# A ninth 2 MB weight slot in a fused two-block kernel, and the first gate half of the experts loaded early

## What is computed

```python
gate = jnp.minimum(xe @ w_gate[e] + b_gate[e], SWIGLU_LIMIT)
up = jnp.clip(xe @ w_up[e] + b_up[e], -SWIGLU_LIMIT, SWIGLU_LIMIT)
act = (up + 1) * (gate * jax.nn.sigmoid(SWIGLU_ALPHA * gate))
return act @ w_down[e] + b_down[e]
```

## Time and profile before

| | |
|---|---|
| median of 3 runs | 1897.9 us (1896.06 to 1900.59) |
| span of the profiled execution | 1896.8 us |
| TensorE busy | 1800.5 us (95%) |
| VectorE, ScalarE busy | 769.7 us (41%), 597.2 us (31%) |
| read from HBM | 560.58 MB |
| first products of the experts, last down products end | 323.5 us, 1250.5 us |

### The profile page before, as it was taken

The page is one execution under the profiler, slowest core; times in us unless marked ns, Lnnn a source line. Parts: engine busy times, 40 slices in busy tenths (PEclk is TensorE's granted clock), DMA queues, the critical chain, the costliest instruction groups (busy, mean ns, idle before and its releaser), DMA issues.

```text
span 1896.8 us, 24863 instructions
## 1 busy us (share of the span) xinstructions
PE 1800.5 (95%) x10374; PEld 1111.5 (59%) x10374; DVE 769.7 (41%) x1339; ACT 597.2 (31%) x1076; POOL 20.4 (1%) x59
## 2 busy tenths in 40 slices
PE   6999999999999999999999999989999999989999
PEld 4987786333333333333333333358799997779998
DVE  2654664231322321222212222154664555646454
ACT  4455564111110111101111011045554445555443
POOL 0020010000000000000000000000000000000000
PEclk9999999999999999999999999999999999999999
DMA  8745446999999999999999999975346464325550
GB/s 306 254 159 192 170 184 262 411 428 426 428 427 427 428 427 427 428 426 428 427 428 428 427 428 428 427 268 178 133 141 207 141 218 160 133 89 179 177 200 23
DMA packets 122050, 563.27 MB, mean 297 GB/s; under 512 B 7216, under 2 KB 53424, under 8 KB 97360
## 3 DMA queue, kind: packets, MB, share of 16 engines
q1 hardware_dynamic: 121104, 558.70, 73.7%
q10 hardware_dynamic: 832, 2.95, 0.4%
HBM read 560.58 MB, written 1.05 MB: 296 GB/s over the span
## 4 chain that ended last, share of the span: by engine, by line
PE 74%; DMA 20%; DVE 3%; ACT 2%; issue 1%; SPq 0%; ACTq 0%; DVEq 0%
PE ps L1082 16%; DMA ring<-in_w_up 13%; PE ps L653 12%; PE ps L654 12%; PE ps L655 12%; PE ps L1117 8%; DMA arena<-in_w_up 5%; PE ps L1023 2%; PE ps L1043 2%; DMA ring<-in_w_ada 1%; PE ps L665 1%; PE ps L971 1%; PE ps L1004 1%; PE ps L758 1%; DMA ring<-in_w_in 1%
## 5 line engine op out<-in xcount | busy, mean ns | idle before, releaser
L653 PE MATMUL ps<-part,part 128*128 128x256 f32 (+2 forms) x1592 | 513.0, 322 | 7.1 <-DVE part L1989 4.3
L654 PE MATMUL ps<-part,part 128*128 128x256 f32 (+2 forms) x1592 | 502.5, 316 | 0.0
L655 PE MATMUL ps<-part,part 128*128 128x256 f32 (+2 forms) x1592 | 502.2, 315 | 0.0
L1082 PE MATMUL ps<-ring,arena 128*64 128x512 f32 x1536 | 342.4, 599 | 30.5 <-DMA ring<-in_w_up 30.2
L1989 DVE TENSOR_TENSOR part<-ring,part 128x1024 fp32r<-128x1024 f32 (+2 forms) x299 | 313.3, 1089 | 122.1 <-ACT part L1449 121.3
L653 PEld LDWEIGHTS ps<-part,part 128*128 128x128 f32 (+1 forms) x1592 | 305.1, 192 | 40.9 <-issue 13.2
L655 PEld LDWEIGHTS ps<-part,part 128*128 128x128 f32 (+1 forms) x1592 | 304.6, 191 | 19.3
L654 PEld LDWEIGHTS ps<-part,part 128*128 128x128 f32 (+1 forms) x1592 | 305.3, 192 | 17.2
L1449 ACT ACTIVATE part<-ring 128x1024 fp32r<-128x1024 f32 (+2 forms) x299 | 271.8, 948 | 32.2 <-PE ps L655 18.9
L1082 PEld LDWEIGHTS ps<-ring,arena 128*64 128x64 f32 x1536 | 115.1, 138 | 255.1 <-issue 254.6
L1986 DVE TENSOR_SCALAR arena<-ps 64x512 f32<-64x512 f32 x128 | 88.2, 689 | 375.9 <-PE ps L1082 370.3
(11 more groups left out here) (250 smaller groups left out, 1190.7 us busy)
## 6 DMA issues: line engine op xcount, KB each, us to landing
ring<-in_w_gate SPq DMA_DIRECT2D x48, 2048.0 KB, 26.4
ring<-in_w_up SPq DMA_DIRECT2D x48, 2048.0 KB, 29.2
ring<-in_w_down SPq DMA_DIRECT2D x48, 2048.0 KB, 27.3
ring<-in_ffn_w_in SPq DMA_DIRECT2D x44, 1024.0 KB, 7.8
arena<-in_w_gate SPq DMA_DIRECT2D x16, 2048.0 KB, 26.3
arena<-in_w_up SPq DMA_DIRECT2D x16, 2048.0 KB, 29.7
arena<-in_w_down SPq DMA_DIRECT2D x16, 2048.0 KB, 27.1
ring<-in_w_ada SPq DMA_DIRECT2D x12, 2048.0 KB, 10.6
```

The lines of the kernel that those rows point to most:

```text
L653: e.matmul(out, x[0], y[0], start=first, stop=False, skip_group_check=True)
L654: e.matmul(out, x[0], y[1], start=False, stop=False, skip_group_check=True)
L655: return e.matmul(out, x[1], y[0], start=False, stop=last, skip_group_check=True)
L1082: i = e.matmul(PS[p + h][CAP * r:CAP * r + CAP, :], xg[:, k0 + k, :], W(("moe_" + "gu"[r], ex, k0))[:, k, 512 * h:512 * h + 512], start=False,
```

## The change

A ninth slot. `spare_slot`, a tile of its own, becomes slot 6, and the two in the arena become 7 and 8. Its 16 KB per partition come from three places: the block of 128 columns of ones in the table of constants (readers now take the single column `one`, with stride 0 where 128 are wanted), 160 columns at the end of the tile `small`, and the scratch of the dynamic DMAs, cut to 1024 bytes. The cycle of the experts is `(6, 4, 0, 3, 5, 2, 1, 7, 8)`, starting behind 6 and 4. The first gate half goes to slot 6, which no one has used, and its load is put in the hand-written list between the `vb` slab and `ada` 6; slot 4, where it was, takes the first up half.

```diff
-for _name, _n in (("ident", 128), ("ones", 128), ("cos2", 128), ...
+for _name, _n in (("ident", 128), ("cos2", 128), ...
...
-        small = sb("small", [128, 640])
+        small = sb("small", [128, 480])
         ringt = sb("ring", [128, NSLOT, SLOT])
+        spare_slot = sb("spare", [128, SLOT])
...
-        more = []
+        more = [spare_slot]
...
-                    ("in", "qb"), ("ada", 5, 1), ("in", "ga0"), ("in", "vb"), ("ada", 6, 0), ("in", "ga1"), ("ada", 7, 1),
+                    ("in", "qb"), ("ada", 5, 1), ("in", "ga0"), ("in", "vb"), ("first", 0, 6), ("ada", 6, 0), ("in", "ga1"), ("ada", 7, 1),
...
-                    ("out", 0, 2), ("o", "ob", 0), ("first", 0, 4), ("out", 1, 1)):
+                    ("out", 0, 2), ("o", "ob", 0), ("first", 1, 4), ("out", 1, 1)):
...
-                plan_rows(("moe_g", 0, 0), A["w_gate"][0][0], 0, key[2])
+                plan_rows(("moe_" + "gu"[key[1]], 0, 0), A[("w_gate", "w_up")[key[1]]][0][0], 0, key[2])
...
-        order = itertools.cycle((4, 0, 3, 5, 2, 1, 6, 7))
+        order = itertools.cycle((6, 4, 0, 3, 5, 2, 1, 7, 8))
         next(order)
-        user[6], user[7] = ("tiles", 6), ("tiles", 7)
+        next(order)
+        user[7], user[8] = ("tiles", 7), ("tiles", 8)
...
-                plan_rows(("moe_u", ex, k0), A["w_up"][0][ex], k0, next(order))
+                    plan_rows(("moe_u", ex, k0), A["w_up"][0][ex], k0, next(order))
...
-                    e.matmul(PS[7][:, 0:2], C("ones")[0:64, :], a.lamt[0:64, 0:2], start=True, stop=True,
+                    e.matmul(PS[7][:, 0:2], C("one", 1, 64).to_broadcast([64, 128]), a.lamt[0:64, 0:2], start=True, stop=True,
...
-    nc = _bacc.Bacc("TRN2", target_bir_lowering=False, num_devices=1)
+    nc = _bacc.Bacc("TRN2", target_bir_lowering=False, num_devices=1, dynamic_dma_scratch_size=1024)
```

More of the change, by code:

```diff
@@ L47 @@
 _at = 0
-for _name, _n in (("ident", 128), ("ones", 128), ("cos2", 128), ("sin2", 128), ("maskT", 256), ("maskD", 128), ("tri", 128),
+for _name, _n in (("ident", 128), ("cos2", 128), ("sin2", 128), ("maskT", 256), ("maskD", 128), ("tri", 128),
                   ("inv", 16), ("eps", 1), ("eps64", 1), ("eps128", 1), ("eps5", 1), ("one", 1), ("iota", 128), ("sel2", 2)):
@@ L62, in shape_constants @@
     put("ident", np.eye(128, dtype=np.float32))
-    put("ones", np.ones((128, 128), np.float32))
     n = np.arange(T)
@@ L190, in tiny @@
             small_at[0] += cols
-            assert small_at[0] <= 640, small_at[0]
+            assert small_at[0] <= 480, small_at[0]
             return a
@@ L214, in build @@
         turn = itertools.count()
-        in_slot, user = [0] * (NSLOT + 2), [None] * (NSLOT + 2)
-        more = []
+        in_slot, user = [0] * (NSLOT + 3), [None] * (NSLOT + 3)
+        more = [spare_slot]
         def plan(key, k, n, pairs_of, slot=None):
@@ L256, in build @@
             else:
-                plan_rows(("moe_g", 0, 0), A["w_gate"][0][0], 0, key[2])
-        s_slot = [signal(f"slot{i}_loaded", 16) for i in range(NSLOT + 2)]
+                plan_rows(("moe_" + "gu"[key[1]], 0, 0), A[("w_gate", "w_up")[key[1]]][0][0], 0, key[2])
+        s_slot = [signal(f"slot{i}_loaded", 16) for i in range(NSLOT + 3)]
         s_used = signal("weights_used")
@@ L611, in rel @@
                 return {3: [s_merged.of(1, 1)], 4: [s_piece.of("a", 35)], 5: [s_mt.of("a", 1)],
-                        6: [s_piece.of("a", 49)], 7: [s_piece.of("a", 49)]}[key[1]]
+                        7: [s_piece.of("a", 49)], 8: [s_piece.of("a", 49)]}[key[1]]
             if kind in ("in", "o", "out"):
@@ L959, in tensor_program @@
             for q in range(2):
-                e.matmul(counts, C("ones", 1), b.G[q], start=q == 0, stop=q == 1, skip_group_check=True)
+                e.matmul(counts, C("one", 1), b.G[q], start=q == 0, stop=q == 1, skip_group_check=True)
             for q in range(2):
-                i = e.matmul(places[:, NE:2 * NE], C(("ones", "tri")[q]), b.G[q], start=q == 0, stop=q == 1, skip_group_check=True)
+                i = e.matmul(places[:, NE:2 * NE], C("tri") if q else C("one", 1).to_broadcast([128, 128]), b.G[q], start=q == 0, stop=q == 1, skip_group_check=True)
             i.then_inc(*s_posn.up())
@@ L1243, in tensor_program @@
                     e.matmul(PS[4][:, 64:68], C("tri"), c.sp[:, 0, 0:4], start=True, stop=True, skip_group_check=True)
-                    e.matmul(PS[4][:, 68:72], C("ones"), c.sp[:, 0, 0:4], start=True, stop=False, skip_group_check=True)
+                    e.matmul(PS[4][:, 68:72], C("one", 1).to_broadcast([128, 128]), c.sp[:, 0, 0:4], start=True, stop=False, skip_group_check=True)
                     e.matmul(PS[4][:, 68:72], C("tri"), c.sp[:, 1, 0:4], start=False, stop=True, skip_group_check=True
```

## The result

The changed kernel was slower: 1911.6 us (median of 6 runs, 1905.3 to 1913.0) against 1898.3 us for the kernel before (6 runs, 1895.8 to 1900.6), a ratio of 1.0060 with an interval of 1.0045 to 1.0075. The time forecast was 1906.8 us, in a range that ends at 1912.0. The sign and the range held, while the median lay 4.8 us above the point, over the upper end of the forecast's own case (1910.3) and 0.4 us inside the range, in the part that was kept for rival C. Measured twice more, beside the kernel before each time, the same kernel gave 1906.3 and 1908.1 us, ratios of 1.0041 and 1.0042. So the first median stood 3.5 to 5.3 us above the later two.

The account below looks back on a forecast made before the run. The prediction took DMA bytes to bound the experts' stretch and TensorE the blocks around it. Its terms, -4.9 + 4.9 + 2.3 + 6.6 = +8.9 us, gave 1906.8 us, in a range of 1898.8 to 1912.0.

Parts of the forecast that it names:

- the forecast's own case: Whole kernel: all terms hold as summed, 1902.9 to 1910.3 us with 1.5 us for two medians; chance 0.62.
- rival C: Experts' stretch: the ninth load early takes nothing off, something besides bytes holds it; +13.8 us, 1911.7; chance 0.10.
- part 1: Experts' DMA-bound stretch: one load fewer remains, so the last lands earlier; -4.9 us.
- part 2: First block: the new load ahead of `ada` 6 makes it land one load later, TensorE waits; +4.9 us.
- part 3: First block, behind the wait for `ada` 6: TensorE runs for a while at a slower clock; +2.3 us.
- part 4: Start of second block: `a_in` 0 must wait for the last down products, delaying ACT's norm; +6.6 us.
- memory edits: Whole kernel: reading the column of ones with stride 0 and the smaller table `con` cost nothing; 0 us.
- A: First block: the lateness at `ada` 6 is made up before the experts; +1.7 us, 1899.6; chance 0.14.
- B: Start of second block: the cost of the late `a_in` 0 is hidden; +2.3 us, 1900.2; chance 0.07.
- D: TensorE catches up what it loses near 103 us and at the second block's start; -4.9 us, 1893.0; chance 0.07.

Follow-up runs that it names:

- the late load: The changed kernel with the early gate half issued behind `ada` 7 instead of ahead of `ada` 6: 1903.4 us, ratio 1.0021 to the kernel before.
- cycle fixed in both: Two kernels with cycle (6, 4, 5, 0, 3, 2, 1, 7, 8): early gate half ahead of `ada` 6, 1899.1 us; behind `ada` 7, 1894.8 and 1896.1 us.
- the load alone: Kernel before, eight slots, memory edits plus an unread 2 MB load ahead of `ada` 6: 1905.0 us, against 1898.5 us without the load.
- the wait alone: Kernel before with one added wait: the load of `a_in` 0 waits for expert 31's last down products. 1904.8 us, ratio 1.0036.
- the freed cycle: The changed kernel with cycle (6, 4, 5, 0, 3, 2, 1, 7, 8), so slot 0 is free earlier: 1899.1 us, ratio 1.0004 to the kernel before.
- first repetition: The changed kernel measured again, unedited, beside the kernel before: 1906.3 us (6 runs), ratio 1.0041.
- both edits together: The changed kernel with the early gate half behind `ada` 7 and cycle (6, 4, 5, 0, 3, 2, 1, 7, 8): 1894.8 and 1896.1 us, ratios 0.9975 and 0.9978.
- the one experiment aimed at it: The changed kernel with three unread products of 128 x 384 in TensorE's gaps near 322 us: 1907.9 us (4 runs), ratio 1.0049.

## Why the prediction was right, step by step

| step | forecast | profiles | medians |
|---|---|---|---|
| part 1, a load fewer | -4.9 | -4.7 | -4.7, -4.2 |
| part 2, `ada` 6 late | +4.9 | +5.0 | with part 3: 3.8 (against the late load), 5.5 and 4.9 (cycle fixed in both), 6.1 (the load alone) |
| part 3, the clock behind it | +2.3 | +1.7 | see part 2 |
| part 4, the seam | +6.6 | +7.2 | 6.8, 7.0, 8.7 |
| memory edits | 0 | | 0.0 |
| sum | +8.9 | +9.2 | +7.8, +8.0 (first measurement +11.4) |

The column on the medians takes differences of ratios (by the two medians themselves the first measurement is +13.3). The column on the profiles compares means over this study's profiles with and without each part. The prediction's other signs came as said, except three: the first expert products came 9.3 us later and not 7, the experts' end 5.9 us later and not 2 (some 4 us of each is the slow stretch near 325), and ACT stood idle for 12 us and not 9 ahead of its two copies. The medians of part 4 come from the wait alone, after against the freed cycle, and the same pair with the load late.

**Part 1** held. From the first expert products to the landing of the last load it takes 918.8 us with eight slots (mean of four profiles, 918.1 to 919.3) and 914.1 with nine (mean of eight, 913.8 to 914.4, without the first profile of after). In that profile it is 915.3, since the first expert still ran at the slow clock.

**Part 2** held. The new load was issued at 89.81, where 89.8 was said, and `ada` 6 landed at 108.7, between the two values worked out, 108.4 and 108.8. The wait was 6.0 us, of which 5.1 are new; the sum took 4.9.

**Part 3** was right in kind and 0.6 us too large (1.0 if the first profile of after, whose slow stretch near 325 lies in this stage, is left out as in part 1: then 221.1 us with the load, +1.3). From the `ada` products to the experts it takes 219.8 us on average without the early load (six profiles) and 221.5 with it (seven). Single profiles spread more than that difference: 218.5 to 221.7 without, 220.3 to 224.0 with. One reason shows in the rows on the clock. In before a slow stretch of 3.4 us came at 174.4; in after and its first repetition there was none at that place. So the new wait did not only add a slow stretch, in some executions an old one was missing. The new one alone cost about 2.1 us, as an estimate from after's profile: TensorE was busy for 4.2 us of it, from 108.8 to 113.0.

**Part 4** was right in mechanism and 0.6 us too small. The term that was mis-sized is the landing of `a_in` 0, taken as 7.9 us from a lone load; it took 9.2, and 9.0 to 9.3 in all the profiles with a late `a_in` 0. This is past the upper bound that I allowed (8.8). One row was too little to take it from: 7.9 is not the fastest (a slab of `w_ada` issued at 66.91 took 7.7), and before's own trace has the very next load of this kind, issued at 1280.50 with the one ahead landed and none behind it for 12 us, at 9.1 us:

```profile
ring<-in_a_w_in SPq DMA_DIRECT2D x1, 2048.0 KB, 9.1
```

The late `a_in` 0 has three more loads issued right behind it. Whether they are what makes it slower than 7.9 was not tested. Two smaller errors took 0.6 us back: from the landing to the root it was 4.2 us, not 4.45, and from the root to the turned rows 0.85, not 1.2. The 0.1 us allowed for an early release of the last down products shows in no run: `a_in` 0 was issued 0.04 us behind their modelled end. DVE's wait ahead of the root vanished as said: ACT goes from the copies straight into the squares. The slow clock behind the seam was paid before too, as said: from the turned rows to the end it took 639.3 us before and 639.7 after. The Trainium skill, page "SBUF — State Buffer", section "The DMA setup-cost knee", has the rule from which the prediction estimated 6.8 us for such a load and 5.5 for the seam. The trace doesn't agree: 9.2 us and 7.2.

**The point and the median.** The sum of the terms, 8.9 us, lies about 1 us above the two later measurements. The first was higher by 3.5 to 5.3 us. Its profile has 4.3 us more than that of the first repetition at one place, the slow clock from 324.7 for 10.2 us: 3.3 us in the products of line 1065 (7.08 against 3.78) and 1.0 in the first expert (14.92 against 13.88). The prediction had no step for this. It is about half of the 8.0 us between the spans of these two profiles, and the rest goes with other slow stretches (54.6 against 34.1 us in all), so the one profile doesn't settle what raised the median. That the first median still fell inside the range is luck: the range reached so far for rival C, not for this. What brings the slow stretch about stays open. The same instructions with the same gaps ran at the full clock in the profiles of the later runs; whether it hangs on the chip or on the time of measurement can't be told from these runs, since the one experiment aimed at it met no such stretch.

**The rivals.** A fell, as the single load in eight slots cost 6.1 us. B fell with the wait alone (+6.8), C with both edits together (-4.7, -4.2), and D with the medians of after, all three above before, and the prices of the two waits. C's price, +13.8, lies close to the 13.3 us by which the first two medians differ. The medians alone would have pointed to it, and the stretch from the first expert products to the last load shows in one profile that the load's gain was there.

## What to carry to other kernels

When a ring of weight slots gets a slot more, count which slot the first load of the next stage falls on and who used it last: here that cost 7 us, more than the slot gained, and another order of the same cycle gave it back. Put an early load where the queue and the engines have nothing urgent behind it, since the loads land in the order of the queue: here the next load came its full 5 us later. And keep copies that wait for a load behind work that doesn't: the order on ACT and DVE was worth about 4 of the 7 us. Last, take the time of a load from all the rows of its kind, not from one.

## What the runs showed of the hardware

A load of 2 MB into idle engines has no single time: the two of the same kind that were issued one by one in before's trace took 7.9 and 9.1 us, and the late `a_in` 0, with three more issued right behind it, 9.0 to 9.3 in seven profiles. SP's own time for issues grows when they come in a row: the four at the seam took it 0.38, 0.58, 3.54 and 4.48 us, single ones elsewhere 0.33 to 0.58.

TensorE's clock is a spread of its own. Over its 23 to 33 runs in a group the kernel before took 1894.7 to 1903.9 us. Of these 80 runs the 20 with a mean clock of 0.993 or more took 1894.7 to 1898.0, and the 18 with 0.988 or less took 1899.0 to 1902.9. Single stretches of 3.4 us at 1.2 GHz stood at other places in other executions (819.5 and 908.3 in before's profile, 826.4 and 1061.9 in after's). The three medians of after, of 5 or 6 runs each, differ by up to 5.3 us, as much as the terms of this sum.
